# Hybrid decoder layer: the second tile's inverse applied once, gate z by tokens, stages moved

## The chip, the cores and the metric

The kernel runs on one core of a Trainium2 chip, in fp32, as one program. The metric is the device time in microseconds (us) of one execution. The engines are TensorE (PE), VectorE (DVE), ScalarE (ACT), GpSimd (POOL) and SyncE (SP), which issues most DMAs. Each has its own instruction queue, run in order, and waits on semaphores.

## The reference, cut to what matters

Batch 1, 256 tokens, width 2048, one layer. A mixing block projects the normed input to u and v (gMLP), to q, k, v and gate z of a gated DeltaNet of 16 heads of 128, to beta and a decay, and to two output gates; then come an output projection, a SwiGLU feed-forward (5632 wide), a per-layer embedding gate and a last norm.

```
h = rms_norm(x, norm_mix);  proj = h @ w_in
q, k, v = silu(causal_conv4(proj_qkv));  q, k = l2norm(q) * dk**-0.5, l2norm(k)
beta = sigmoid(dn_beta);  g = -exp(a_log) * softplus(dn_a + dt_bias)
# gated delta rule, chunks, g summed within a chunk
m    = strict_lower((k*beta) @ k.T * decay);  inverse = (1 + m)^-1
u_c  = inverse @ (v*beta);  w_c = inverse @ (k*beta*exp(g))
v_new = u_c - w_c @ state
o     = (q*exp(g)) @ state + (q @ k.T * decay) @ v_new
state = state*exp(g_last) + k_tail.T @ v_new
o = rms_norm(o, dn_out_norm) * silu(z)
merged = gate_a * (y_a @ w_a) + gate_b * (o @ w_b);  x = x + merged @ w_out
x = x + (silu(f_gate) * f_up) @ w_down;  x = x + ple_gate * (p @ w_ple);  rms_norm(x)
```

## The kernel before, in words

**Weights.** Every large matrix streams from HBM in *halves* of 512 KB, 604 in all, through a ring of four slots. For each half ACT makes a rounded high part (`split_hi`, L287) and DVE the remainder (`split_lo`, L295), three halves ahead of their use. TensorE multiplies the high weights by high and low activations at once (512 columns: 256 tokens high, 256 low) and the low weights by the high activations (256 columns). The result for columns of output features lies with features on partitions, its high and low sums side by side (`times_high` L302, `times_low` L307). With `rows=True` the tokens lie on partitions and the weights move, 512 wide (L320, L325): 12 matmuls for a half instead of 16. Where nothing else stands between them, halves go in pairs (`use_pair`): both high parts, then both low parts. A finished block leaves PSUM in two steps: ACT copies the low sum (`low_part`, L982), DVE adds the high sum (L1420), and for q, k, v, z DVE multiplies by R, the reciprocal root of the mean square of each token.

**Phases.** v (16 halves, tokens on partitions), then four head groups (`group`, 32 halves each: k, q, v, z of four heads, two blocks of four halves each), u (16), four rounds of mix (gate a, gate b, branch a, branch b), out, ffn, down, proj, ple. In phase v PE also makes the products for beta and decay (`beta_a`, L624, 16 fp32 matmuls on x times the norm's gain) behind half 12, and right behind it puts R on partitions (L628).

**The order of the small work** is written out by hand. `FINISH`, `START`, `CONV`, `EARLY` and `YS` are tables, one set for each engine: the number is the half of the running group behind which (PE) or with whose split (ACT, DVE) a stage stands. `START` holds stages of the group whose keys are just made, `FINISH` those of the group before. On ACT and DVE the split comes first, then the stages.

**Delta rule.** Two tiles of 128 tokens for each of four heads. PE makes the Gram matrices (`gram_m` L681, behind half 14), DVE scales them (`make_negm` L1521), ACT stores the 32x32 diagonal blocks and loads them back in another layout (`store_m`, `load_m` L1125), POOL inverts them in 62 small steps (`invert`, L509 and L511), ACT stores and loads the result (`store_x`, `load_diag`), and in the next group PE merges the blocks to the full inverse (`merge32_a` behind half 5, to `merge64_b` behind half 8). Then: `first_tile` behind 9 (inverse times weighted values, and inverse times weighted keys `kbeg`, four products each), `carry` behind 10, `second_tile` behind 11 (for each head inverse times values plus `nwT` times state), `outputs` behind 12. The outputs are squared (POOL), their root taken (ACT, `o_rt`), scaled (DVE, `o_scale` L1576, one instruction), turned (PE, `turn_o` L789, behind half 20), and multiplied by the gain and by silu(z) (DVE, `norm_o` L1583). The query-key product `gram_q` (L691) stands behind half 20 and waits for the query's SiLU (ACT L1036).

For the last group the finishing stages run in phase u and at the start of mix: `o_scale` with the last u half, `turn_o` behind mix half 0, the spatial products (`spatial`, L838) behind mix half 2.

Of the kernel before, what the change touches and what calls it, by code (L numbers as in the profile page):

```python
# [13 lines left out]


# [5 lines left out]
F32 = mybir.dt.float32  # L21
# [25 lines left out]
WARM = 16  # L47
# [30 lines left out]
E0, _e = {}, 0  # L78
for _name, _n in (("qkvz", 8 * NGROUPS), ("u", 4), ("mix", 4 * NB), ("ffn", 2 * FB)):
    E0[_name] = _e  # L80
    _e += _n
# [13 lines left out]
def build(nc, win, wba, wa, wb, wo, wgu, wd, wpg, wpp, xT_d, pT_d, cols_d, hv_d, gmw_d, gmb_d, fin_d, out_d):  # L95
# [33 lines left out]
    kbeg = shared("kbeg", [P, GROUP, P], F32, 40)  # L129
# [17 lines left out]
    nwT = shared("nwT", [P, GROUP, P], F32, 81)  # L147
    state = shared("state", [P, GROUP, P], F32, 83)
    vg = xT[:].rearrange("p k n -> p (k n)")[:, 0:TILES * GM].rearrange("p (m n) -> p m n", m=TILES)
    uT = shared("uT", [P, GMT, SEQ], F32, 28)  # L150
# [4 lines left out]
    wba_sb = shared("wba_sb", [P, KD, 48], F32, 62)  # L155
    g1 = shared("g1", [48, SEQ], F32, 71)
# [48 lines left out]
    def heads(flat, width):  # L205
# [15 lines left out]
    consts_made, wba_scaled = sem("consts_made"), sem("wba_scaled")  # L221
# [12 lines left out]
    q_meaned, k_turned, k_summed, k_rooted, v_weighed = (sem("q_meaned"), sem("k_turned"), sem("k_summed"), sem("k_rooted"),  # L234
                                                         sem("v_weighed"))
# [15 lines left out]
    z_scaled, z_silu, yb_hi, yb_lo = sem("z_scaled"), sem("z_silu"), sem("yb_hi"), sem("yb_lo")  # L251
# [48 lines left out]
    def times_high(o, s, kt, m, x, k, begin):  # L300

        nc.tensor.matmul(o, whi[:, s, kt, m * P:(m + 1) * P], x[:, k].rearrange("p q n -> p (q n)"), start=begin, stop=False,  # L302
                         skip_group_check=True)

    def times_low(o, s, kt, m, x, k, end):

        return nc.tensor.matmul(o[:, 0:SEQ], wlo[:, s, kt, m * P:(m + 1) * P], x[:, k, 0], start=False, stop=end,  # L307
                                skip_group_check=True)

    def use_half(pe, phase, i, n, buf, first, last, h, x, rows=False, into=acc):  # L310
# [16 lines left out]
        else:  # L327
            pe.wait_ge(hi_done, half_of(phase, i, n) + 1)
            for kt in range(HALF_K):
                for m in range(2):  # L330
                    times_high(acc[buf][:, m], s, kt, m, x, HALF_K * h + kt, first and kt == 0)
            pe.wait_ge(lo_done, half_of(phase, i, n) + 1)
            for kt in range(HALF_K):
                for m in range(2):
                    mm = times_low(acc[buf][:, m], s, kt, m, x, HALF_K * h + kt, last and kt == HALF_K - 1)
        mm.then_inc(half_used, 1)

    def use_pair(pe, phase, i, n, buf, first, last, h, x):

        for p in range(2):  # L340
            pe.wait_ge(hi_done, half_of(phase, i, n + p) + 1)
            for kt in range(HALF_K):
                for m in range(2):
                    times_high(acc[buf][:, m], (n + p) % RING, kt, m, x, HALF_K * (h + p) + kt, first and p == 0 and kt == 0)
        for p in range(2):
            pe.wait_ge(lo_done, half_of(phase, i, n + p) + 1)
            for kt in range(HALF_K):
                for m in range(2):
                    mm = times_low(acc[buf][:, m], (n + p) % RING, kt, m, x, HALF_K * (h + p) + kt,
                                   last and p == 1 and kt == HALF_K - 1)  # L350
            mm.then_inc(half_used, 1)
# [46 lines left out]
    with nc.Block() as block:  # L398
# [58 lines left out]
        def _(pool):  # L457
# [35 lines left out]

            pool.wait_ge(cols_in, 16)
            pool.wait_ge(ba_in, 32)
            g.tensor_tensor(wba_sb[:], wba_sb[:], bc(cols[:, C_MIX:C_MIX + KD], 48), ALU.mult).then_inc(wba_scaled, 1)

            INV_STEPS = 63

# [1417 lines left out]
```

## Time and profile before

| | us |
|---|---|
| median of 3 runs | 1814.24 (1812.48 to 1818.14) |
| the profiled execution | 1817.25 |
| its span | 1815.6 |
| DVE busy | 1166.4 (64%) |
| ACT busy | 882.1 (49%) |
| POOL busy | 257.5 (14%) |

```profile
## 2 busy tenths in 40 slices
PE   9999999999999999999999999999999999999998
PEld 8788888888888888888888888888888888888887
DVE  6587797787957655665667555555555555545556
ACT  6664454545546444444445444444444443434455
POOL 4016152161621000000010000000000000000002
PEclk9999999999999999999999999999999999999999
```

Each digit is one fortieth of the span (45 us), in tenths; PEclk is the clock that was granted to TensorE. The head groups lie in slices 2 to 12; from about 600 us on only the large products are left. A matmul's own span overlaps the next one's, so a stretch of PE is measured from start to start.

### The profile page before, as it was taken

The numbers are of one execution on the slowest core, as the hardware profiler recorded it, in microseconds if no ns is written. First come the engines' busy times: TensorE is split into PE (matmuls) and PEld (weight loads), VectorE is DVE, ScalarE is ACT, GpSimd is POOL, SyncE is SP. The second block draws the span as 40 slices with busy tenths as digits, with TensorE's granted clock in tenths as the row PEclk, the third lists the DMA queues.
The fourth block names the chain that finished last, engine by engine and source line by source line (L and its number), as shares of the span: only waits on it lengthen the run. The fifth ranks groups of instructions, "written<-read, shape, count | busy, mean of one in ns | idle before, by whom it ended". The sixth has DMA issues, their size and how long they took to land.

```text
span 1815.6 us, 29811 instructions
## 1 busy us (share of the span) xinstructions
PE 1794.4 (99%) x10662; PEld 1580.9 (87%) x10662; DVE 1166.4 (64%) x1415; ACT 882.1 (49%) x1040; POOL 257.5 (14%) x367
## 2 busy tenths in 40 slices
PE   9999999999999999999999999999999999999998
PEld 8788888888888888888888888888888888888887
DVE  6587797787957655665667555555555555545556
ACT  6664454545546444444445444444444443434455
POOL 4016152161621000000010000000000000000002
PEclk9999999999999999999999999999999999999999
DMA  7456456464565565555555555555555556565653
GB/s 256 156 173 188 143 155 192 129 189 139 176 188 188 188 195 192 180 190 196 176 184 195 190 191 192 189 190 185 186 192 188 185 184 203 172 206 175 224 180 130
DMA packets 103848, 332.64 MB, mean 183 GB/s; under 512 B 23184, under 2 KB 23328, under 8 KB 103520
## 3 DMA queue, kind: packets, MB, share of 16 engines
q1 hardware_dynamic: 88592, 320.57, 54.0%
q10 hardware_dynamic: 14096, 5.07, 1.3%
q0 software_dynamic: 1088, 6.03, 0.9%
q8 instruction: 47, 0.77, 0.2%
q14 instruction: 25, 0.20, 0.0%
HBM read 328.46 MB, written 3.16 MB: 183 GB/s over the span
## 4 chain that ended last, share of the span: by engine, by line
PE 88%; DVE 6%; issue 2%; ACT 2%; ACTq 1%; DVEq 0%; DMA 0%; POOL 0%; POOLq 0%
PE acc L302 50%; PE acc L307 26%; PE acc L320 4%; PE acc L325 2%; DVE wlo L295 2%; ACT whi L287 1%; DVE negm L1521 0%; PE acc L916 0%; PE acc L915 0%; PE acc L914 0%; DVE conv_k L1452 0%; DVE conv_q L1452 0%; PE ps L646 0%; PE ps L624 0%; DVE pre L1420 0%
## 5 line engine op out<-in xcount | busy, mean ns | idle before, releaser
L295 DVE TENSOR_TENSOR wlo<-raw,whi 128x1024 fp32r<-128x1024 f32 x604 | 750.0, 1267 | 517.4 <-ACT whi L287 513.6
L287 ACT ACTIVATE whi<-raw 128x1024 fp32r<-128x1024 f32 x604 | 623.7, 1055 | 579.9 <-PE acc L307 504.7
L302 PE MATMUL acc<-ax,whi 128*128 128x512 f32 x3072 | 754.5, 394 | 0.9 <-ACTq L1178 0.9
L302 PEld LDWEIGHTS acc<-ax,whi 128*128 128x128 f32 x3072 | 560.4, 189 | 106.9 <-ACTq L1178 1.1
L307 PEld LDWEIGHTS acc<-ax,wlo 128*128 128x128 f32 x3072 | 404.6, 191 | 22.0 <-DVE wlo L295 0.4
L307 PE MATMUL acc<-ax,wlo 128*128 128x256 f32 x3072 | 411.2, 283 | 0.0
L302 PE MATMUL acc<-fx,whi 128*128 128x512 f32 x704 | 172.5, 392 | 0.0
L302 PEld LDWEIGHTS acc<-fx,whi 128*128 128x128 f32 x704 | 128.0, 189 | 23.6
L565 POOL TENSOR_TENSOR sqsum<-sqsum,t 128x512 f32<-128x512 f32 x16 | 22.1, 1380 | 632.2 <-ACT t L1307 632.2
L307 PEld LDWEIGHTS acc<-fx,wlo 128*128 128x128 f32 x704 | 93.5, 191 | 5.3
L509 POOL TENSOR_TENSOR blk_t<-blk_m,blk_x 128x60 f32<-128x60 f32 (+24 forms) x124 | 71.3, 575 | 169.3 <-DMA blk_m<-inv_in 159.9
L307 PE MATMUL acc<-fx,wlo 128*128 128x256 f32 x704 | 95.1, 283 | 0.0
L573 POOL TENSOR_TENSOR t<-t,R 128x512 f32<-128x512 f32 x22 | 28.7, 1305 | 449.5 <-ACT t L1320 449.5
L320 PE MATMUL acc<-whi,ax 128*128 128x512 f32 x320 | 81.6, 398 | 0.0
L320 PEld LDWEIGHTS acc<-whi,ax 128*128 128x128 f32 x320 | 60.9, 192 | 12.6
L511 POOL TENSOR_TENSOR blk_x<-blk_x,blk_t 128x60 f32<-128x60 f32 (+24 forms) x124 | 66.3, 535 | 9.7
L302 PE MATMUL acc<-mx,whi 128*128 128x512 f32 x256 | 62.6, 392 | 0.0
L302 PE MATMUL acc<-yb,whi 128*128 128x512 f32 x256 | 61.4, 391 | 0.0
L1420 DVE TENSOR_TENSOR t<-acc,t 128x512 f32<-128x512 f32 x80 | 54.7, 684 | 10.4 <-ACT t L982 10.4
L982 ACT ACTIVATE t<-acc 128x512 f32<-128x512 f32 x80 | 47.5, 594 | 22.6 <-PE acc L307 19.3
L302 PEld LDWEIGHTS acc<-yb,whi 128*128 128x128 f32 x256 | 46.9, 188 | 9.0
L302 PEld LDWEIGHTS acc<-mx,whi 128*128 128x128 f32 x256 | 46.6, 189 | 8.6
(273 smaller groups left out, 1342.9 us busy)
## 6 DMA issues: line engine op xcount, KB each, us to landing
raw<-in_win SPq DMA_DIRECT2D x224, 512.0 KB, 3.6
raw<-in_wgu SPq DMA_DIRECT2D x176, 512.0 KB, 4.1
raw<-in_wd SPq DMA_DIRECT2D x88, 512.0 KB, 4.0
raw<-in_wb SPq DMA_DIRECT2D x32, 512.0 KB, 4.0
raw<-in_wo SPq DMA_DIRECT2D x32, 512.0 KB, 4.4
raw<-in_wpg SPq DMA_DIRECT2D x32, 512.0 KB, 3.6
raw<-in_wa SPq DMA_DIRECT2D x16, 512.0 KB, 4.7
blk_m<-inv_in ACTq DMA_DIRECT2D x16, 128.0 KB, 4.3
```

Source lines behind the costliest of these rows:

```text
L287: nc.scalar.activation(whi[:, s], raw[:, s], ACT.Copy).then_inc(hi_done, 1)
L295: nc.vector.tensor_tensor(wlo[:, s], raw[:, s], whi[:, s].bitcast(F32), ALU.subtract).then_inc(lo_done, 1)
L302: nc.tensor.matmul(o, whi[:, s, kt, m * P:(m + 1) * P], x[:, k].rearrange("p q n -> p (q n)"), start=begin, stop=False, skip_group_check=True)
L307: return nc.tensor.matmul(o[:, 0:SEQ], wlo[:, s, kt, m * P:(m + 1) * P], x[:, k, 0], start=False, stop=end, skip_group_check=True)
L320: nc.tensor.matmul(into[buf][:, m], x[:, WIDE_K * h + kt, q, m * P:(m + 1) * P], whi_w[:, s, kt], start=first and kt == 0 and q == 0, stop ...
L325: mm = nc.tensor.matmul(into[buf][:, m], x[:, WIDE_K * h + kt, 0, m * P:(m + 1) * P], wlo_w[:, s, kt], start=False, stop=last and kt == WI ...
L509: chain(g.tensor_tensor(tmp, blk_m[:, j + 1:32, j:j + 1].to_broadcast([P, r, c]), blk_x[:, j:j + 1, 0:c].to_broadcast([P, r, c]), ALU.mult ...
L511: chain(g.tensor_tensor(blk_x[:, j + 1:32, 0:c], blk_x[:, j + 1:32, 0:c], tmp, ALU.add), v + 3 + 2 * j)
L565: g.tensor_tensor(sqsum[:], sqsum[:], piece(t[1], q % 2), ALU.add).then_inc(s["added"], 1)
L573: g.tensor_tensor(piece(t[1], j), piece(t[0], j), over(R[:], 2), ALU.mult).then_inc(ff_gate, 1)
L982: f(dst, accv[buf][:, :, 1], ACT.Copy).then_inc(low_taken, 1)
L1420: v.tensor_tensor(dst, accv[buf][:, :, 0], dst, ALU.add).then_inc(part_summed, 1)
```

## The change

- *Second tile.* `kbeg`, `nwT` and their products are gone. The keys of the second tile are copied aside by POOL (`keep_k`); a new stage `keys_state` behind half 11 multiplies them by the state, DVE adds that times a (now negative) weight to the weighted values (`less_state`), and `second_tile`, now behind half 12, applies the inverse once. `outputs` goes to 13.
- *Gate z* is computed with tokens on partitions (`rows=True`, weights laid out so on the host), in two blocks that each cover half of the input width, added by DVE. SiLU takes R as its scale; `o_scale` multiplies by root and gate in eight instructions; `norm_o` becomes a scaled copy on ACT, behind the turn.
- *Beta* in the split format: ACT and DVE split the small weights, PE makes 16 matmuls of 512 columns and 112 rows on the split activations; R's columns come before half 12 instead of behind the beta product.
- *Pairs* take turns in which part goes first; *warm-up* is 5 matmuls of 512 columns instead of 16 of 64.
- *Stages moved*, as the tables show.

```diff
-WARM = 16
+WARM = 5
-                mm(psf[1][:, 64 * n:64 * n + 64], ones[:], ones[:, 0:64], start=True, stop=True)
+                mm(ps[1][:, n % 2], ones[:], over(ones[:], 4), start=True, stop=True)
...
-            for n in range(0, halves - 1, 2):
-                    use_pair(pe, phase, i, n0 + n, buf, n == 0, n + 2 == halves, n, x)
+            for n in range(0, halves - 1, 2):
+                    use_pair(pe, phase, i, n0 + n, buf, n == 0, n + 2 == halves, n, x, low_now())
+        if low_first:
+            low(first, False)
+            high(False, last)
+        else:
+            high(first, False)
+            low(False, last)
+    def low_now():
+        return next(turns) % 2 == 1
...
-                pe.wait_ge(wba_scaled, 1)
+                pe.wait_ge(wba_split, 2)
                 for k in range(KD):
-                    last = mm(psf[1][0:48, 0:SEQ], wba_sb[:, k], xT[:, k], start=(k == 0), stop=(k == KD - 1))
+                    last = mm(ps[1][0:112, 0], wsp[:, k], ax[:, k].rearrange("p q n -> p (q n)"), start=(k == 0), stop=(k == KD - 1))
+            def r_columns():
                 pe.wait_ge(r_done, 1)
...
+            def keep_k(n):
+                pool.wait_ge(conv_silu, n)
+                g.tensor_copy(kend[:], conv[1][:, :, P:SEQ]).then_inc(k_kept, 1)
...
             def first_tile(d):
...
-                for h in range(GROUP):
-                    last = mm(psq[1][:, 4 + h], kbeg[:, h], invT[:, 4 + h], start=True, stop=True)
+            def keys_state(d):
+                pe.wait_ge(k_kept, d + 1)
+                pe.wait_ge(delta_dve, 2 * d + 1)
+                for h in range(GROUP):
+                    last = mm(psq[1][:, 4 + h], kend[:, h], state[:, h], start=True, stop=True)
             def second_tile(d):
                 pe.wait_ge(delta_dve, 2 * d + 2)
                 for h in range(GROUP):
-                    mm(psq[0][:, 4 + h], invT[:, 4 + h], vbeta[:, 4 + h], start=True, stop=False)
-                    last = mm(psq[0][:, 4 + h], nwT[:, h], state[:, h], start=False, stop=True)
+                    last = mm(psq[0][:, 4 + h], invT[:, 4 + h], vbeta[:, 4 + h], start=True, stop=True)
+            def less_state(d):
+                for h in range(GROUP):
+                    x = v.scalar_tensor_tensor(vbeta[:, 4 + h], psq[1][:, 4 + h], kr[:, 2, 1, h:h + 1], vbeta[:, 4 + h], ALU.mult, ALU.add)
...
@@ tables of TensorE
-                      11: second_tile, 12: outputs, 20: turn_o}
-            EARLY = {20: gram_q}
-            START = {12: turn_k, 14: gram_m, 27: lambda g: (turn_q(g), transpose_v(g))}
+                      11: keys_state, 12: second_tile, 13: outputs, 22: turn_o}
+            EARLY = {22: gram_q}
+            START = {13: turn_k, 15: gram_m, 28: lambda g: (turn_q(g), transpose_v(g))}
+                    if p < 6:
+                        gemm("qkvz", g, p * HID, HID, p % 2, p // 2, ax, after=after)
+                    else:
+                        gemm("qkvz", g, p * HID, HID, p % 2, p // 2, ax, rows=True, after=after, h0=(p - 6) * HID)
-            gemm("v", 0, HWIDE, HWIDE, 1, 0, ax, rows=True, after={1: first_sum, 4: beta_a})
+            gemm("v", 0, HWIDE, HWIDE, 1, 0, ax, rows=True, after={1: first_sum, 3: r_columns, 4: beta_a})
-            mix(0, after={0: lambda: turn_o(NGROUPS - 1), 2: spatial})
+            mix(0, after={1: lambda: turn_o(NGROUPS - 1), 2: spatial})
@@ tables of ScalarE
-            FINISH = {1: (silu_z1,), 2: (store_x,), 3: (load_diag,), 6: (copy_p32,), 7: (copy_inv,), 10: (copy_v0,), 12: (copy_v1,),
-                      13: (copy_o,), 15: (o_rt,)}
-            START = {10: (silu_k,), 11: (decay_m,), 13: (square_k,), 15: (k_root,), 16: (store_m,), 17: (load_m,), 18: (silu_q,),
-                     20: (g_exp, decay_q), 25: (silu_v,), 28: (square_q,), 29: (silu_z0,)}
+            FINISH = {1: (silu_z,), 2: (store_x,), 3: (load_diag,), 6: (copy_p32,), 7: (copy_inv,), 10: (copy_v0,), 13: (copy_v1,),
+                      14: (copy_o,), 16: (o_rt,), 23: (norm_o,)}
+            START = {10: (silu_k,), 11: (decay_m,), 14: (square_k,), 16: (k_root,), 17: (store_m,), 18: (load_m, silu_q),
+                     20: (g_exp, decay_q), 25: (silu_v,), 29: (square_q,)}
+                if b == 3:
+                    act.wait_ge(o_mean, 3 * NGROUPS - 2)
-            YS = {0: (lambda: yb_high(1),), 1: (lambda: yb_high(2),), 5: (lambda: ya_high(0),),
+            YS = {0: (lambda: o_rt(NGROUPS - 1), lambda: yb_high(1)), 1: (lambda: yb_high(2),), 2: (lambda: norm_o(NGROUPS - 1),), 5: (lambda: ya_high(0),),
-                if n == 14:
+                if n == 13:
+                    ba_part()
                     v_block(0)
@@ VectorE
+                for h in range(GROUP):
+                    for m in range(TILES):
+                        o = t[2][:, h, m * P:(m + 1) * P]
+                        x = v.scalar_tensor_tensor(o, o, length[:, 2, 2 * h + m:2 * h + m + 1], zt[:, m, h * P:(h + 1) * P],
+                                                   ALU.mult, ALU.mult)
-                      9: (copy_invT64,), 10: (copy_nwT,), 11: (copy_state,), 14: (o_inv,), 18: (o_scale,), 21: (norm_o,)}
-            START = {10: (diff_m,), 14: (k_scale,), 15: (make_negm,), 17: (diff_q,), 22: (decay_q,), 25: (make_qkT,), 28: (scale_v,),
-                     29: (q_mean,)}
-            CONV = {5: conv_a(1, 0), 8: conv_b(1, 0), 14: conv_a(0, 1), 16: conv_b(0, 1), 21: conv_a(2, 2), 24: conv_b(2, 2)}
+                      9: (copy_invT64,), 11: (copy_state,), 12: (less_state,), 15: (o_inv,), 18: (o_scale,)}
+            START = {10: (diff_m,), 15: (k_scale,), 16: (make_negm,), 17: (diff_q,), 22: (decay_q,), 24: (make_qkT,), 29: (scale_v,),
+                     30: (q_mean,)}
+            CONV = {5: conv_a(1, 0), 9: conv_b(1, 0), 14: conv_a(0, 1), 16: conv_b(0, 1), 21: conv_a(2, 2), 24: conv_b(2, 2)}
-                if n == 15:
-                    o_scale(NGROUPS - 1)
-            YS = {0: (lambda: yb_low(1),), 1: (lambda: norm_o(NGROUPS - 1),), 3: (sv_bias,),
+            YS = {0: (lambda: yb_low(1), lambda: o_scale(NGROUPS - 1)), 3: (sv_bias,),
```

## Rows read from the trace of the kernel before

**Rows 1.** Busy times of the whole span: busy us (share of the span) xinstructions, by engine.

```profile
PE 1794.4 (99%) x10662; PEld 1580.9 (87%) x10662; DVE 1166.4 (64%) x1415; ACT 882.1 (49%) x1040; POOL 257.5 (14%) x367
```

**Rows 2.** Waits of TensorE: line waited for, us in total, times, longest us.

```profile
PE ps L691 <- ACT conv_q L1036: 6.8, 4, 4.0
PE ps L752 <- DVE invT L1554: 1.3, 3, 0.4
...
PE ps L838 <- DVE oT L1583: 1.0, 1, 1.0
PE acc L302 <- ACTq L1178: 0.9, 1, 0.9
```

**Rows 3.** Timeline of TensorE, phase v: start us, us, engine, line, operation.

```profile
21.39 1.98 PE L320 MATMUL acc<-whi,ax 128*128 128x512 f32 x8
...
24.11 1.98 PE L320 MATMUL acc<-whi,ax 128*128 128x512 f32 x8
```

**Rows 4.** Timeline of TensorE, last u block and first mix half, columns.

```profile
559.97 2.00 PE L302 MATMUL acc<-ax,whi 128*128 128x512 f32 x8
...
562.76 1.03 PE L789 MATMUL ps<-ident,t 128*128 128x128 f32 x8
```

**Rows 5.** Timeline of TensorE in the feed-forward, pairs of halves.

```profile
1034.54 3.82 PE L302 MATMUL acc<-ax,whi 128*128 128x512 f32 x16
...
1040.10 1.09 PE L302 MATMUL acc<-ax,whi 128*128 128x512 f32 x4
```

**Rows 6.** Timeline of TensorE, the beta product.

```profile
46.87 7.11 PE L624 MATMUL ps<-xT,wba_sb 128*48 128x256 f32 x32
```

**Rows 7.** Timeline of ScalarE, the root that makes R.

```profile
44.80 0.42 ACT L977 ACTIVATE R<-Rt 128x256 f32<-128x256 f32 x1 [2.26 <-DVE Rt L1402]
```

**Rows 8.** Timeline of TensorE, group 2, second tile and the half behind it.

```profile
322.17 0.39 PE L769 MATMUL ps<-vbeta,invT 128*128 128x128 f32 x2
...
323.87 1.40 PE L302 MATMUL acc<-ax,whi 128*128 128x512 f32 x5
```

**Rows 9.** Timeline of VectorE, group 2, half 12 and the scaled Gram matrix.

```profile
324.44 1.22 DVE L295 TENSOR_TENSOR wlo<-raw,whi 128x1024 fp32r<-128x1024 f32 x1
...
344.31 2.16 DVE L1521 SCALAR_TENSOR_TENSOR negm<-ps,kr,negm 128x128 f32<-128x128 f32 x8
```

**Rows 10.** Timeline of TensorE, group 2, query-key product and transpose.

```profile
355.21 2.05 PE L691 MATMUL ps<-conv_q,conv_k 128*128 128x128 f32 x16 [0.60 <-ACT conv_q L1036]
357.58 1.09 PE L789 MATMUL ps<-ident,t 128*128 128x128 f32 x8 [0.32 <-DVE t L1576]
```

**Rows 11.** Timeline of TensorE, group 0, the query-key product.

```profile
129.75 3.78 PE L691 MATMUL ps<-conv_q,conv_k 128*128 128x128 f32 x16 [3.97 <-ACT conv_q L1036]
```

**Rows 12.** Stretch behind it: us, busy PE PEld DVE ACT POOL, PEclk, DMA share, GB/s.

```profile
130.00:136.00 6.00, 6.00 (x23) 5.42 (x24) 3.82 (x5) 5.88 (x7) 5.04 (x11) 0.51 0.60 182
```

**Rows 13.** Timeline of ScalarE, group 0, issue of the block loads.

```profile
124.42 1.75 ACTq L1125 DMA_DIRECT2D blk_m<-inv_in  x4
```

**Rows 14.** Timeline of ScalarE, last u block.

```profile
558.51 1.28 ACT L1110 ACT_TABLE_LOAD   x1
...
565.40 1.05 ACT L1239 ACTIVATE yb<-oT 128x1024 fp32r<-128x1024 f32 x1
```

**Rows 15.** Timeline of ScalarE, group 2, issue of the block loads.

```profile
349.79 1.74 ACTq L1125 DMA_DIRECT2D blk_m<-inv_in  x4
```

**Rows 16.** Timeline of GpSimd, group 2, from the blocks' arrival to the diagonal's.

```profile
356.06 2.64 POOL L509 TENSOR_TENSOR blk_t<-blk_m,blk_x 128x31 f32<-128x31 f32 x1 [23.09 <-DMA blk_m<-inv_in]
...
364.28 0.27 POOL L509 TENSOR_TENSOR blk_t<-blk_m,blk_x 128x52 f32<-128x52 f32 x1
...
408.12 1.45 POOL L518 COPY invT<-diagT 32x256 f32<-32x256 f32 x1 [10.65 <-DMA diagT<-inv_out]
```

**Rows 17.** Timeline of TensorE, first merge behind group 2.

```profile
408.10 1.07 PE L713 MATMUL ps<-diagT,negm 32*32 32x32 f32 x32
```

**Rows 18.** Timeline of VectorE, group 2, o_scale.

```profile
356.24 1.22 DVE L1576 TENSOR_TENSOR t<-t,length 128x1024 f32<-128x1024 f32 x1
```

More of the change, by code:

```diff
@@ L327, in use_half @@
         else:
[L328 to L335, printed above, removed]
-        mm.then_inc(half_used, 1)
@@ L338, in use_pair, with high @@
[L338 to L351, printed above, removed]
+            def high(begin, end):
+                pe.wait_ge(hi_done, half_of(phase, i, n) + 1)
+                for kt in range(HALF_K):
+                    for m in range(2):
+                        mm = times_high(acc[buf][:, m], s, kt, m, x, HALF_K * h + kt, begin and kt == 0, end and kt == HALF_K - 1)
+                return mm
@@ new lines, in low @@
+            def low(begin, end):
+                pe.wait_ge(lo_done, half_of(phase, i, n) + 1)
+                for kt in range(HALF_K):
+                    for m in range(2):
+                        mm = times_low(acc[buf][:, m], s, kt, m, x, HALF_K * h + kt, begin and kt == 0, end and kt == HALF_K - 1)
+                return mm
+            if low_first:
+                low(first, False)
+                mm = high(False, last)
+            else:
+                high(first, False)
+                mm = low(False, last)
@@ new lines, in use_half, with use_pair, high, low @@
+        mm.then_inc(half_used, 1)
+    def use_pair(pe, phase, i, n, buf, first, last, h, x, low_first):
+        def high(begin, end):
+            for p in range(2):
+                pe.wait_ge(hi_done, half_of(phase, i, n + p) + 1)
+                for kt in range(HALF_K):
+                    for m in range(2):
+                        mm = times_high(acc[buf][:, m], (n + p) % RING, kt, m, x, HALF_K * (h + p) + kt,
+                                        begin and p == 0 and kt == 0, end and p == 1 and kt == HALF_K - 1)
+                if low_first:
+                    mm.then_inc(half_used, 1)
+        def low(begin, end):
+            for p in range(2):
+                pe.wait_ge(lo_done, half_of(phase, i, n + p) + 1)
+                for kt in range(HALF_K):
+                    for m in range(2):
+                        mm = times_low(acc[buf][:, m], (n + p) % RING, kt, m, x, HALF_K * (h + p) + kt,
+                                       begin and p == 0 and kt == 0, end and p == 1 and kt == HALF_K - 1)
+                if not low_first:
+                    mm.then_inc(half_used, 1)
+        if low_first:
+            low(first, False)
+            high(False, last)
+        else:
+            high(first, False)
+            low(False, last)
@@ L353, in acc_free @@
+    turns = itertools.count()
+    def low_now():
+        return next(turns) % 2 == 1
     def acc_free(pe, phase, i, buf, n):
```

165 lines of the change are left out of this document (98 added, 67 removed).

## The prediction

> **What bounds the kernel now.** I read the page's busy times first, then TensorE's waits, then its timeline. TensorE (PE) works for 1794.4 of 1815.6 us [rows 1]: the time is the sum of its matmuls, and a change pays only if it takes matmul time out of PE or closes one of its gaps. The gaps in the middle are few: 6.8 us before the query-key product of the four head groups, 1.3 before the first-tile product, 1.0 before the spatial products, 0.9 at a buffer [rows 2]. What the change does on VectorE (DVE), ScalarE (ACT) and GpSimd (POOL) counts only through such gaps. The profiled execution took 1817.25 us (span 1815.6); the median of the runs is 1814.24, 3.0 lower. I sum against 1817.25 and take the same difference from 1814.24. Halves (512 KB of weights) are numbered within a head group, 0 to 31; "on the old clock" means in the times of the trace.
>
> **A half.** With rows of tokens it takes 24.11-21.39 = 2.72 us [rows 3], with columns 562.76-559.97 = 2.79 [rows 4], in a pair 1040.10-1034.54 = 5.56, 2.78 each [rows 5]. A switch between high and low products costs about 0.01.
> - *Gate z by tokens:* 32 halves x 0.07 = **-2.3**.
> - *Pairs that take turns in which part comes first:* 159 pairs lose one of two switches, -1.7. A low-first pair needs its second low half 1 us after its start instead of 4.6 us; no row shows such a half late, but behind a block's evacuation it is the last thing that DVE makes. Between a loss of 2 and all of the 1.7, I take **-1.0**.
>
> **The beta product.** Sixteen fp32 products took 7.04 us [rows 6]. Sixteen of 512 columns in the split format, at the rate of rows 3 (2.72/12 = 0.227), take 3.6: -3.4. But the columns of R now come ahead of half 12 of this phase, which began at 46.87-2.8 = 44.1, and R is there only at 45.22, released by DVE and not by PE [rows 7]: +1.2. With an extra stage switch of 0.1 the sum is **-2.1**. This wait also absorbs what the five wide warm-up products do to the start: between 1.5 late and 2.5 early, both are gone at 45.2. The first value block's activation moves one half earlier on ACT, so the buffer of [rows 2] is free 3 us sooner: its 0.9 goes, with 0.1 of restart, **-1.0**.
>
> **Second tile.** Eight products take 323.87-322.17 = 1.70 us [rows 8], so four fewer save 0.85, less a stage switch of 0.1: four times 0.8 is -3.2. Against it stands a new wait. Keys times state would end at 322.17+0.85 = 323.0 on the old clock and half 12 at 325.9; the four products behind it wait for the subtraction, which DVE begins after the split that ends at 325.66. Four instructions of L1521's kind (2.16/8 = 0.27 each) make it 326.8 [rows 9]: 0.9, four times, +3.6 (0 were DVE ahead, 4.5 were they slower). Behind the waiting products stands only PE's own queue, so all of it is time. Net **+0.3** with rounding. The first-tile product waits for a copy that now comes before the key convolution on DVE instead of behind it: 1.3 us in three groups [rows 2] plus restarts, **-1.8**.
>
> **The query-key product** moves from behind half 20 to behind half 22, 5.6 us. In groups 1 to 3 the 2.8 us of wait go. The product also stretches there, 357.58-355.21 = 2.37 for what takes 1.70, the transpose's 0.32 within it [rows 8, 10]; I count 0.7 for each: **-5.0**. In group 0 the wait was 3.97 us [rows 11], and the clock granted behind it 0.51, the lower level of 1.2 GHz, for 6 us [rows 12]: 3 us of work lost. Those 7.0 go. But between its splits for halves 21 and 22 ACT now issues the block loads and runs the query's SiLU. The issue began at 124.42 and took 1.75 [rows 13]. Its input is now made behind an evacuation and a split more on DVE (1.4 and 1.2, by columns from rows 9) and without kbeg (-0.7), so 126.3. With 1.75, a table load of 1.28, the SiLU and the split, 1.05 each [rows 14], half 22 has its high part at 131.4; PE wants it at 129.75-3.97+2.8 = 128.6. That is +2.8, or 1.4 if the stores land faster; I take 2.3, too short to bring the clock down. Net **-4.7**.
>
> **The inversion's chain.** From the load's issue at 349.79 [rows 15] the chain runs through POOL (from 356.06) to the diagonal blocks at 408.12 [rows 16], and PE starts on them at 408.10 [rows 17]: no slack in this group. The change makes the load 1.0 to 1.9 us later here (the count of group 0; I take 1.0, since DVE is not filled throughout) and PE 2.2 earlier (gaps closed 1.6, z 0.6): 3.2 us of new wait per group, if POOL stays as slow. It doesn't quite: POOL's first step took 2.64 us while DVE ran tensor_tensors such as L1576 [rows 18], against 0.27 beside convolutions of scalar_tensor_tensors [rows 16]. The change turns L1576 (1.22) into eight of the latter and drops two z scalings (1.4), so up to 2.6 come back. I take 0.8 in group 2 and 0.3 each in groups 1 and 3: **+1.4**, between 0 and 10.
>
> The Trainium skill, "SBUF — State Buffer", section "Who interferes with whom", says that any VectorE instruction with two inputs in SBUF keeps GpSimd's reads out, not only a tensor_tensor. By it the eight new o_scale instructions would block POOL for 2.2 us where the old one took 1.2, the chain would be some 2 us longer than in my sum in two groups, and the saving 4 us smaller. The trace speaks against it with the steps of 0.27 us beside convolutions that read SBUF twice.
>
> **The last group's outputs.** Here the change costs. turn_o moves one half on, to 562.76+2.79 = 565.55 on the old clock [rows 4]. The scaling that it waits for moves further: the outputs are made a half later, o_rt follows the last u block's GELU and a split on ACT, with a table load, and o_scale on DVE stands behind yb_low(1), which waits for yb_high(1) on ACT. yb_high(1) began at 565.40 behind the same GELU and split; a table load of 1.28 and the root (0.2) now come before it: from 566.9 to 568.0 [rows 14]. DVE's yb_low(1), as wide as L1576, adds 1.2 [rows 18] and o_scale 8 x 0.27 = 2.15 [rows 9]: 571.3. PE waits 571.3-565.5 = 5.8 us. A wait of 3.97 lowered the clock and cost 3.0 more [rows 11, 12]; I add 3.0. The 1.0 before the spatial products goes [rows 2], since norm_o is on ACT, half a stage ahead of them. Net **+7.8**, between -1.1 (scaling in time) and +9.
>
> **Sum.** -2.3 -1.0 -2.1 -1.0 +0.3 -1.8 -5.0 -4.7 +1.4 +7.8 = -8.4 us: 1817.25 becomes 1808.9 in a profiled execution, 1814.24 becomes 1805.8. The z scaling, kbeg, nwT and norm_o that leave DVE and the key copy that POOL gets are put at nothing: PE's matmuls cover them, as they cover the 1166.4 us that DVE is busy [rows 1]; POOL's copy stands ahead of square_o and ends before its input is there. Without that cover the copy would cost its 0.7 to 1.4 per group.
>
> **Rivals.**
> - *A, the last outputs come in time* (a wait under 2 us, clock untouched): 7 to 9 us better, 1797.5. For it: ACT's and DVE's queues have idle time there. Against it: both run in order, and yb_high(1) already began at 565.40. 0.24.
> - *B, POOL gives the chain nothing back:* 3 x 3.2 instead of 1.4, 8.2 worse, 1814.0. For it: no slack at 408.10. Against it: 2.64 against 0.27 [rows 16]. 0.16.
> - *C, slower: the clock falls at the chain.* The place is PE's wait for diagT behind half 5 of each group. At 3.2 us it stands 0.8 short of the wait of rows 11; if the load comes 1.9 later instead of 1.0, it passes it, and each of three waits costs 0.9 and 3.0 more: 1814.0+11.7 = 1825.7. 0.08.
> - *D, the second SBUF input blocks POOL* (eight instructions of 0.27): 1805.8+4.2 = 1810. Against it: the 0.27 of rows 16. It is the skill's rule of the section named above. 0.07.
> - *The forecast*, 1800 to 1809.5: 0.45.
>
> **The numbers.** 0.3%, 5.4 us, is about what a measurement can tell from no change, so the limits are 1808.8 and 1819.7. Faster: A and most of the forecast, 0.69. Same: B, D, the forecast's edge, 0.22. Slower: C and what I don't see, 0.09. The range takes in the better part of A and all of B: 1794 to 1814.5.
>
> **What would show it.** Right: L691 is gone from TensorE's waits or below 0.5; there is one wait of 5 to 6 us near 560 before the transpose of the last outputs, with a granted clock of half behind it; 0.9 four times before the second tile, on DVE's subtraction; 1.2 before the columns of R; 1.4 to 3 for a high half in group 0; z halves at 2.72. Wrong: no wait before that transpose (A); merge32_a waiting 3 us for its transfer in three groups (B), with half a clock behind it (C); low halves waited for in the pairs.

## The result

The changed kernel takes 1807.09 us (median of 5 runs, 1804.78 to 1808.35), the kernel before beside it 1817.38 (median of 5). The ratio is 0.9947, with a 95% interval of 0.9928 to 0.9966. The profiled execution took 1808.35 us against 1817.25, 8.9 less; 8.4 was forecast.

Busy times of the whole span, which answer to [rows 1]:

```profile
PE 1782.1 (99%) x10464; PEld 1563.5 (87%) x10464; DVE 1169.4 (65%) x1442; ACT 887.1 (49%) x1041; POOL 251.6 (14%) x371
```

TensorE is busy for 12.3 us less and waits 3.4 us more. Its waits, which answer to [rows 2] (line waited for, us in total, times, longest us):

```profile
PE ps L839 <- DVE t L1657: 6.2, 1, 6.2
PE ps L820 <- DVE vbeta L1639: 3.4, 4, 0.8
PE ps L759 <- DMA diagT<-inv_out: 1.6, 2, 1.4
PE acc L329 <- DVE wlo L299: 1.4, 1, 1.4
PE acc L324 <- ACT whi L291: 1.3, 2, 1.1
...
PE ps L674 <- ACT R L1032: 1.1, 1, 1.1
```

The query-key product's wait of 6.8 us is gone. In its place stand 6.2 before the last transposes, four of 0.8 before the second tile, and 1.6 for the diagonal blocks. At the start, 1.3 for high halves and 1.1 for R (L324, L674) take in whatever differs before them, and 1.4 for a low half (L329) lies in group 0.

**The sum, term by term.** All 4880 high products stand in the same order in both traces, so I compared the starts of the same halves and gave what exceeds an undisturbed half to the product or wait beside it (times in us):

| term | forecast | measured |
|---|---|---|
| gate z by tokens | -2.3 | -2.3 |
| pairs that take turns | -1.0 | -1.6 |
| beta product, with the wait for R | -2.1 | -1.8 |
| buffer of the first value block | -1.0 | -1.1 |
| second tile | +0.3 | +1.2 |
| first tile's copy | -1.8 | -2.4 |
| query-key product, groups 1 to 3 | -5.0 | -6.1 |
| query-key product, group 0 | -4.7 | -5.7 |
| the inversion's chain | +1.4 | +3.2 |
| the last group's outputs | +7.8 | +7.9 |
| sum | -8.4 | -8.7 |

The starts of the last halves differ by 8.9; the rest is rounding and what no term names.

The timeline of TensorE (start us, us, engine, line, operation) gives each term. A gate half with tokens as rows takes 140.73-138.01 = 2.72, as [rows 3]:

```profile
138.01 1.98 PE L324 MATMUL acc<-whi,ax 128*128 128x512 f32 x8
...
140.73 1.98 PE L324 MATMUL acc<-whi,ax 128*128 128x512 f32 x8
```

The columns of R wait for ACT, then half 12 and the beta product in the split format follow; 52.74-49.06 = 3.68 stands against the 7.04 of [rows 6]:

```profile
45.67 0.60 PE L674 MATMUL ps<-ones,R 1*128 1x1 f32 x4 [1.06 <-ACT R L1032]
...
49.06 3.84 PE L667 MATMUL ps<-ax,wsp 128*112 128x512 f32 x16
52.74 1.98 PE L324 MATMUL acc<-whi,ax 128*128 128x512 f32 x8
```

In group 2, keys times state takes 0.81, and the second tile's products come 0.85 late; they answer to [rows 8]. The column in brackets is the wait before the row:

```profile
310.30 1.05 PE L813 MATMUL ps<-state,kend 128*128 128x128 f32 x8
...
315.00 1.16 PE L820 MATMUL ps<-vbeta,invT 128*128 128x128 f32 x8 [0.85 <-DVE vbeta L1639]
```

On VectorE the split of step 12 (L299) stands ahead of the subtraction, which ends at 314.94 (compare [rows 9]):

```profile
312.69 1.21 DVE L299 TENSOR_TENSOR wlo<-raw,whi 128x1024 fp32r<-128x1024 f32 x1
313.83 1.11 DVE L1639 SCALAR_TENSOR_TENSOR vbeta<-ps,kr,vbeta 128x128 f32<-128x128 f32 x4
```

In group 0 the query-key product starts without a wait ([rows 11]: 3.97):

```profile
127.96 1.95 PE L737 MATMUL ps<-conv_q,conv_k 128*128 128x128 f32 x16
```

ScalarE issued the block loads at 119.79 and ran the query's SiLU at 122.87 ([rows 13]: 124.42 for the issue):

```profile
119.79 1.76 ACTq L1183 DMA_DIRECT2D blk_m<-inv_in  x4
...
122.87 1.06 ACT L1094 ACTIVATE conv_q<-conv_q 128x1024 f32<-128x1024 f32 x1
```

The first inversion's diagonal blocks come 1.38 late, in the second group. The high half behind them takes 180.54-177.12 = 3.42 instead of 1.96; in that stretch the granted clock is 0.62 on the mean (columns as in [rows 12]), since it stood at 0.5, the lower level of 1.2 GHz, from 176.9 to 180.3:

```profile
176.05 1.14 PE L759 MATMUL ps<-diagT,negm 32*32 32x32 f32 x32 [1.38 <-DMA diagT<-inv_out]
177.12 3.58 PE L306 MATMUL acc<-ax,whi 128*128 128x512 f32 x8
180.54 1.11 PE L311 MATMUL acc<-ax,wlo 128*128 128x256 f32 x8
```

```profile
176.00:180.50 4.50, 4.45 (x40) 3.73 (x41) 4.50 (x10) 2.06 (x5) 2.77 (x4) 0.62 0.45 146
```

Before the last transposes TensorE waits 6.19. They take 558.39-556.77 = 1.62 instead of 0.79 and the half behind them 3.56 instead of 1.94, at half the clock, for 6.8 us in all:

```profile
556.77 1.97 PE L839 MATMUL ps<-ident,t 128*128 128x128 f32 x8 [6.19 <-DVE t L1657]
558.39 3.76 PE L306 MATMUL acc<-ax,whi 128*128 128x512 f32 x8
```

On ScalarE the root (L1168) stands behind the GELU, a split and a table load, and yb_high(1) (L1308) behind it; on VectorE yb_low(1) (L1773) is ahead of the eight scalings (L1657), which end at 556.7. This is the chain that the prediction drew from [rows 14]:

```profile
550.91 1.28 ACT L1168 ACT_TABLE_LOAD   x1
552.20 0.21 ACT L1168 ACTIVATE length<-length 128x8 f32<-128x8 f32 x1
552.32 1.04 ACT L1308 ACTIVATE yb<-oT 128x1024 fp32r<-128x1024 f32 x1
```

```profile
553.39 1.23 DVE L1773 TENSOR_TENSOR yb<-oT,yb 128x1024 fp32r<-128x1024 f32 x1 [1.24 <-ACT yb L1308]
554.53 2.18 DVE L1657 SCALAR_TENSOR_TENSOR t<-t,length,xT 128x128 f32<-128x128 f32 x8
```

### The profile page after: what moved, and what is told of

It is laid out like the page before. It is cut to its first block, busy times and chain, and to the rows that moved or that the text cites. A ratio compares the mean times of both kernels' runs of the same rounds, so it can differ in the third digit from the quotient of the medians.

```text
span 1806.7 us, 29541 instructions
## 1 busy us (share of the span) xinstructions
PE 1782.1 (99%) x10464; PEld 1563.5 (87%) x10464; DVE 1169.4 (65%) x1442; ACT 887.1 (49%) x1041; POOL 251.6 (14%) x371
## 4 chain that ended last, share of the span: by engine, by line
PE 89%; issue 2%; DVE 2%; POOL 2%; DMA 2%; ACT 1%; ACTq 0%; POOLq 0%; DVEq 0%; SPq 0%
PE acc L306 49%; PE acc L311 26%; PE acc L324 6%; PE acc L329 3%; DMA raw<-in_win 1%; POOL blk_x L544 1%; DVE wlo L299 1%; POOL blk_t L542 1%; ACT whi L291 1%; DMA inv_out<-blk_xT 0%; PE acc L971 0%; PE acc L970 0%; PE acc L969 0%; DMA diagT<-inv_out 0%; PE ps L737 0%
## 5 line engine op out<-in xcount | busy, mean ns | idle before, releaser
L299 DVE TENSOR_TENSOR wlo<-raw,whi 128x1024 fp32r<-128x1024 f32 x604 | 749.4, 1265 | 513.8 <-ACT whi L291 507.7
L306 PE MATMUL acc<-ax,whi 128*128 128x512 f32 x2816 | 682.4, 394 | 0.0
L306 PEld LDWEIGHTS acc<-ax,whi 128*128 128x128 f32 x2816 | 518.7, 189 | 101.4
L311 PEld LDWEIGHTS acc<-ax,wlo 128*128 128x128 f32 x2816 | 363.1, 191 | 15.1
L311 PE MATMUL acc<-ax,wlo 128*128 128x256 f32 x2816 | 367.6, 283 | 0.0
L324 PE MATMUL acc<-whi,ax 128*128 128x512 f32 x576 | 143.9, 392 | 1.3 <-ACT whi L291 1.3
L324 PEld LDWEIGHTS acc<-whi,ax 128*128 128x128 f32 x576 | 107.0, 188 | 24.6 <-ACT whi L291 2.2
L329 PE MATMUL acc<-wlo,ax 128*128 128x512 f32 x288 | 77.4, 391 | 1.4 <-DVE wlo L299 1.4
L542 POOL TENSOR_TENSOR blk_t<-blk_m,blk_x 128x60 f32<-128x60 f32 (+24 forms) x124 | 63.8, 514 | 102.0 <-DMA blk_m<-inv_in 92.6
L329 PEld LDWEIGHTS acc<-wlo,ax 128*128 128x128 f32 x288 | 53.8, 188 | 13.8 <-DVE wlo L299 2.7
```

Of the source, the lines that this page charges most:

```text
L299: nc.vector.tensor_tensor(wlo[:, s], raw[:, s], whi[:, s].bitcast(F32), ALU.subtract).then_inc(lo_done, 1)
L306: return nc.tensor.matmul(o, whi[:, s, kt, m * P:(m + 1) * P], x[:, k].rearrange("p q n -> p (q n)"), start=begin, stop=end, skip_group_ch ...
L324: nc.tensor.matmul(into[buf][:, m], x[:, WIDE_K * h + kt, q, m * P:(m + 1) * P], whi_w[:, s, kt], start=first and kt == 0 and q == 0, stop ...
L329: mm = nc.tensor.matmul(into[buf][:, m], x[:, WIDE_K * h + kt, 0, m * P:(m + 1) * P], wlo_w[:, s, kt], start=False, stop=last and kt == WI ...
L542: chain(g.tensor_tensor(tmp, blk_m[:, j + 1:32, j:j + 1].to_broadcast([P, r, c]), blk_x[:, j:j + 1, 0:c].to_broadcast([P, r, c]), ALU.mult ...
```

## The experiments

Every kernel but the last two is the changed kernel with one edit. Whole times of one kernel spread by up to 4.6 us (1799.57 to 1804.21 for the second experiment). The traces also differ at the start (R's wait is between 0.7 and 1.1) and in the first inversion, for a reason that stays open below. So what an edit does is read at its place, from the starts of the same halves, and the medians stand beside it.

### The last scaling early

```
 ScalarE, last u block:   u_part(3)
+                         o_rt(NGROUPS - 1)
                          u_block(3)
 VectorE:                 u_block(3)
+                         o_scale(NGROUPS - 1)
 (both taken out of step 0 of the first mix)
```

> From the changed kernel (1808.35 us profiled); only the last head group's root and scaling are issued earlier: the root ahead of the last u block's GELU on ACT, the scaling right behind that block's evacuation on DVE. Theory (the wait of 6.19 us before the last transposes comes from the order in ACT's and DVE's queues, and the low clock behind it from the wait): the input of the root is there at 546.7, ACT is free at 547.1, a table load and the root end at 548.6, the evacuation at 549.3, eight scalings end at 551.5, and TensorE is there at 550.6: the wait becomes 0.9 and the 2.75 us of low clock go, -8.0 us. Rival 1 (the low clock belongs to the eight short transposes and the spatial products, not to the wait): -5.3. Rival 2 (the split behind the GELU, now a table load later, takes the wait's place): -3 to -5.

Measured: 1798.37 us, ratio to the kernel before 0.9895 (0.9879 to 0.9912). At its place it saves 8.05 us. The wait is 0.84. The root ends at 548.0, a table load is paid twice, and the scalings, begun at 548.60, end at 550.8:

```profile
546.51 1.28 ACT L1168 ACT_TABLE_LOAD   x1
547.80 0.21 ACT L1168 ACTIVATE length<-length 128x8 f32<-128x8 f32 x1
548.03 1.28 ACT L1301 ACT_TABLE_LOAD   x1
```

```profile
548.60 2.18 DVE L1658 SCALAR_TENSOR_TENSOR t<-t,length,xT 128x128 f32<-128x128 f32 x8
```

No low clock follows, so the 2.75 us of low clock belonged to the wait. The order of two queues, not their load, cost the change half of what it could have given.

### The last transposes one half later

```
-mix(0, after={1: lambda: turn_o(NGROUPS - 1), 2: spatial})
+mix(0, after={2: lambda: turn_o(NGROUPS - 1), 3: spatial})
 (norm_o on ScalarE and the bias on VectorE one half later as well)
```

> From the changed kernel; nothing is made earlier, but TensorE transposes the last outputs one half later (and the spatial products, ACT's norm and DVE's bias move with it). Theory (the scaling is ready at 556.7 whatever TensorE does): TensorE comes 2.8 us later, the wait is 3.4 instead of 6.19, -2.8; the low clock behind it, 2.75 us, stays, since a wait of 4.2 us brought it in the kernel before. Rival (the clock falls only behind the longer wait): -5.5. Either way the norm on ACT must not delay a split; if it does, up to 1 us is lost again.

Measured: 1803.07 us, ratio 0.9915 (0.9899 to 0.9932), -3.9 at its place, between the two. (The wait of the kernel before, 4.2 in the expectation, is 3.97 in [rows 11].) The wait is 3.40, as forecast, and the clock does fall behind it, but for 3.4 us instead of 6.8: the transposes take 1.62 as before, the half behind them 2.69 instead of 3.56.

```profile
556.57 1.97 PE L839 MATMUL ps<-ident,t 128*128 128x128 f32 x8 [3.40 <-DVE t L1657]
558.19 2.85 PE L306 MATMUL acc<-ax,whi 128*128 128x512 f32 x8
```

### Pairs without turns

```
 def low_now():
-    return next(turns) % 2 == 1
+    return False
```

> From the changed kernel; in the pairs of halves the high products always come first, as before the change. Theory (a change between high and low products costs 0.01 us each, and there are 159 pairs): +1.6 us, spread evenly from 565 us to the end, which is what the two traces differ by there. Rival (the 1.6 us comes from other things behind 565): 0.

Measured: 1807.51 us, ratio 0.9943 (0.9926 to 0.9959). Between the first pair and the end it loses 1.65 us to the changed kernel. All of the term comes from the switches, and no low half was waited for.

### The subtraction ahead of its split

```
 for n in range(GH):
+    if n == 12:
+        less_state(g - 1)
     split_lo(dve, "qkvz", g, n)
 (the same in phase u for the last group; taken out of step 12)
```

> From the changed kernel; DVE makes the subtraction for the second tile ahead of the split of half 12 instead of behind it, in all four groups. Theory (the 0.85 us that TensorE waits before the second tile is DVE's order: the split of 1.21 stands ahead of the subtraction, and its result is not wanted before 3 us later): the four waits go, -3.4 us. Rival (DVE is the limit there, and the wait moves to the low half behind): 0.

Measured: 1802.25 us, ratio 0.9915 (0.9898 to 0.9931). The second tile's wait is gone from the list of waits, and the stage costs 0.90 instead of 2.00 in each group: -4.4. That is 1.0 more than the four waits of 0.85: each wait costs 0.25 beside its own length, 0.10 of it in the product behind it.

### The columns of R behind the beta product

```
-after={1: first_sum, 3: r_columns, 4: beta_a}
+after={1: first_sum, 3: beta_a, 4: r_columns}
 (ScalarE's v_block(0) from step 13 to 14, VectorE's copy of R behind its step for beta)
```

> From the changed kernel; TensorE makes the beta product ahead of the columns of R instead of behind them, and ACT's activation of the first value block goes back one half. Theory (two terms of the sum hang together): the wait for R, 0.8 to 1.1 us in the five traces so far, is covered by the product's 3.7 us and goes; the value block's buffer comes free a half later and the buffer wait of the kernel before, 1.0 with its restart, is back: 0.0 in sum. Rival (the buffer wait went for another reason): -1.0 us.

Measured: 1806.35 us, ratio 0.9943 (0.9926 to 0.9961). The wait for R is gone (-1.1 at half 13), and the buffer's is back, 1.0 before half 4 of group 0; with restarts the kernel stands 0.3 behind the changed one at half 12 of that group. The two terms hang together. What came on top was not expected: group 0 then lost 1.2 us more, and in the second group the wait for the diagonal blocks fell to 0.3, with no low clock, so that the trace ends 2.0 before the changed kernel's:

```profile
PE acc L306 <- ACTq L1244: 1.0, 1, 1.0
...
PE ps L759 <- DMA diagT<-inv_out: 0.3, 1, 0.3
```

### The first inversion's store early

```
 for n in range(GH):
+    if n == 16:
+        make_negm(0)
     split_lo(dve, "qkvz", 0, n)
```

> From the changed kernel; in the first head group alone DVE makes the matrix that is stored for the inversion ahead of the split of half 16 instead of behind it. Theory (TensorE's wait of 1.4 to 1.7 us for the diagonal blocks in the second group, and the low clock of 3.4 us behind it, come from the first group's inversion, whose chain begins at this store): the store and all behind it come 1.2 us earlier, the wait shrinks to 0.2 to 0.5 and the low clock is gone: -1.2 -1.5 = -2.7 us. Rival 1 (the low clock needs no wait of this size): -1.2. Rival 2 (the chain is paced by ACT's place in its queue, not by the store): 0.

Measured: 1807.06 us, ratio 0.9953 (0.9937 to 0.9968). The four loads were issued at 119.90 (119.79 in the changed kernel), and one of the four issues took 1.8 us instead of 0.45; ScalarE's split behind it came late and TensorE waited 1.8 for it. The inversion ended at 163.6 instead of 166.4, since its 62 steps took 35.6 us instead of 37.2, and the wait for the diagonal blocks went with its low clock (-3.0 in the second group). Group 0 lost 2.5, so the net is -0.5 at these places. So the low clock does hang on that wait, but the edit didn't move the load, as the second rival had it.

### The second key convolution back

```
-CONV = {5: conv_a(1, 0), 9: conv_b(1, 0), ...
+CONV = {5: conv_a(1, 0), 8: conv_b(1, 0), ...
```

> From the changed kernel; the second key convolution goes back from behind step 9 to behind step 8 on DVE, so that the copy of the inverse for the first tile waits behind it again. Theory (the first tile's 1.7 us in the kernel before against 0.9 were this wait): +0.8 in three head groups, +2.4 us. Rival (the copy would be in time anyway): 0.

Measured: 1806.68 us, ratio 0.995 (0.9932 to 0.9969), which tells nothing by itself. At its place the first tile costs 0.50, 0.70 and 0.69 more in the three groups, with waits of 0.25 to 0.44: +1.9. The move accounts for 1.9 of the 2.4 measured. Most of the other 0.5 is no wait for this copy: in the last group, where TensorE waited for nothing there, the stage is shorter too, by 0.9 for the four products that the term counts at 0.8.

### The query-key product back

```
-EARLY = {22: gram_q}
+EARLY = {20: gram_q}
```

> From the changed kernel; TensorE's query-key product goes back from behind half 22 to behind half 20, everything else as changed. Theory (most of the 11.8 us that this step gave comes from ACT's and DVE's order, which has the query's activation ready at 123.9, 235.1, 343.8 and 452.8, and not from TensorE's move): TensorE would be there at 122.4, 234.9, 343.7 and 452.7: waits of 1.6, 0.2, 0.1 and 0.1, and one stage switch of 0.09 more in three groups, together +2.3 us. Rival (the move on TensorE is what gave it): +8 us or more, with the low clock back in the first group.

Measured: 1805.94 us, ratio 0.994 (0.9919 to 0.996). TensorE waits 1.47, 0.06 and 0.22 there, and no low clock follows. Over halves 20 to 29 that is +0.3, +0.3, +0.5 and +0.3: 1.4 of the 11.8 us. The other 10.4 came from what this run left as changed. On ScalarE and VectorE that is the order: in group 0 the SiLU began at 128.64 in the trace of before, and at 122.87+2.97 = 125.84 on the same clock in the changed kernel. On TensorE it is the two stages of transposes that also stand later (turn_o behind half 22, those of the query and the value behind half 28). The share of each step was not tried. As a whole the kernel came out 2.4 faster than the changed one: the first inversion ended 3.9 earlier (162.5), its wait with the low clock was gone (-3.0), and the start was 0.6 earlier.

### Every split on VectorE as a scalar_tensor_tensor

```
-tensor_tensor(wlo, raw, whi, subtract)
+scalar_tensor_tensor(wlo, whi, -1.0, raw, mult, add)
```

> From the changed kernel; every split on DVE is one scalar_tensor_tensor (high part times -1 plus the weights) instead of one tensor_tensor, of the same 1024 elements, with the same two inputs in SBUF. Theory (as in the prediction: a tensor_tensor keeps GpSimd out, a scalar_tensor_tensor doesn't): the steps of the inversion beside a split fall from 0.9 us to 0.36, the 37.2 us from its first to its last step to about 28, and the wait for the diagonal blocks in the second group goes with its low clock, -3 us, if the split itself is not slower. Rival (any DVE instruction with two inputs in SBUF keeps GpSimd out as long as it runs, and the steps beside the convolutions are short because each of those runs for 0.4 us only): the steps stay at 0.9 and the inversion at 37, 0 us.

Measured: 1804.73 us, ratio 0.9933 (0.9912 to 0.9955). The mean of GpSimd's steps that lie mostly beside a split is 0.91 us (85 steps; 0.92 over 83 in the changed kernel), and the first inversion takes 37.2 us, as before. In the timelines of VectorE and GpSimd two steps beside the six convolutions, of 0.48 us each, take 0.38 and 0.40, and the one that meets the long scalar_tensor_tensor takes 1.24:

```profile
251.24 2.88 DVE L1529 SCALAR_TENSOR_TENSOR conv_v<-pre,cols,conv_v 128x256 f32<-128x256 f32 x6
254.04 1.36 DVE L299 SCALAR_TENSOR_TENSOR wlo<-whi,raw 128x1024 fp32r<-128x1024 f32 x1
```

```profile
253.46 0.38 POOL L544 TENSOR_TENSOR blk_x<-blk_x,blk_t 128x64 f32<-128x64 f32 x1
253.92 0.40 POOL L542 TENSOR_TENSOR blk_t<-blk_m,blk_x 128x75 f32<-128x75 f32 x1
254.40 1.24 POOL L544 TENSOR_TENSOR blk_x<-blk_x,blk_t 128x75 f32<-128x75 f32 x1
```

The rival holds: what counts is that two inputs lie in SBUF, and how long the instruction runs. Beside L1583 of the kernel before, a scalar_tensor_tensor of 1.28 us with one input in PSUM, nine steps took 0.29 on the mean. (Of the 3.9 us that this trace ends earlier than the changed kernel's, 2.1 are the second group, where the wait was 0.6 with no low clock, and 1.4 lie behind the last transposes, where the low clock began 4 us before the wait's end instead of 1.)

### The old warm-up

```
-WARM = 5, products of 512 columns
+WARM = 16, products of 64 columns
```

> From the changed kernel; the warm-up is again 16 narrow products instead of 5 wide ones. Theory (what the warm-up gives to the start is absorbed by the wait for R, which DVE releases): the first half starts at 8.0 on the lower clock, 3.56 us for its high products, the full clock comes near 13, and half 13 still starts at 52.4 to 52.8, 0.0 us. Rival (the wide warm-up gives the start 2.3 us): +2.3 us.

Measured: 1806.58 us, ratio 0.9941 (0.9921 to 0.9961). The full clock comes at 10.4 instead of 6.2, the first high products take 3.02 instead of 1.93, and half 13 starts at 52.28: 52.74 in the changed kernel, 51.87 to 52.36 in the four kernels of the first experiments, which start as it does. Its trace ends 2.2 before the changed kernel's: half 13 came 0.5 earlier, group 0 lost 1.75, and the second group's wait for the diagonal blocks was gone with its low clock (-3.0). The edit was not aimed at these. The warm-up gives nothing that the wait for R doesn't take.

### Three fixes together

The last scaling early, the subtraction ahead of its split, and the query-key product behind half 20; then the same with that product behind half 21.

> From the changed kernel (1808.35 us profiled); the last scaling early, the subtraction ahead of its split, and the query-key product behind half 20, together. Theory (the three act in different places and add up): -8.1 -4.3 -2.4 = -14.8, 1793.5 us profiled, with one wait of 0.8 before the last transposes, 1.5 before the first group's query-key product, none before the second tile, and no low clock until the last microseconds. Rival (TensorE, 1.1 us earlier in each group, meets the inversion's chain again): one to three waits of 1 us before the diagonal blocks, with low clock behind them, 1796 to 1800.

> As the run with the three fixes, but the query-key product stands behind half 21. Theory (the query's activation is ready at 123.9 in the first group and TensorE is there at 125.2; the wait of 1.5 goes, but DVE, which caught up in that wait, is then late for half 27 again, and the first inversion's load meets the traffic that it met with the product behind half 22): 0 to +3 us against the three fixes. Rival (only the wait counts): -1.4 us against them.

Measured: 1793.72 us (1793.55 to 1794.10), ratio 0.987 (0.9851 to 0.989), and 1793.06 us, ratio 0.9865 (0.9845 to 0.9884). The first is 14.8 below the changed kernel at the last halves, as forecast; both beat both kernels. What is left of TensorE's waits in the first: the query's SiLU, high halves at the start, the warm-up's ones and the last scaling, and 0.8 for R.

```profile
PE ps L737 <- ACT conv_q L1094: 1.8, 3, 1.5
...
PE ps L839 <- DVE t L1658: 0.8, 1, 0.8
```

The second is 0.2 below it in the traces and 0.7 in the medians. In group 0 neither place is better: the wait of 1.5 is gone and 1.5 for a low half at half 27 has come. In groups 1 to 3 half 21 is the better place by 0.4 each; a start that came 0.8 later hides most of this in the whole trace. Neither the theory (0 to +3) nor the rival (-1.4) had it.

## Why the prediction was right

The time was right within 0.5 us of the profiled difference (8.4 against 8.9; in medians 1805.8 against 1807.09), and so was the mechanism of its biggest term. The terms behind it were off by up to 1.8, and that they cancelled is luck.

- **The last outputs** (+7.8; 7.9): wait 6.2 against 5.8, low clock 2.75 against 3.0. The wait and its cause are shown by the early scaling, which takes back 8.05, and the clock's share by the disappearance of the low clock with it. Rival A was wrong because ScalarE and VectorE kept the order in which the steps were issued, though both had idle time; the same idle time made it cheap to mend.
- **Gate z, buffer, beta** were right within 0.3. That R's wait absorbs the start is shown by the old warm-up, and that it stands against the buffer by the swap.
- **Pairs** (-1.0; -1.6): all switches paid and no low half was late. The doubt that I priced at 0.7 didn't come true.
- **Second tile** (+0.3; +1.2): four waits of 0.85 were forecast at 0.9, and its cause is shown. With the wait closed the term is 1.2-4.4 = -3.2, which is what I had for the products; what I missed is the 0.25 that each wait costs beside its length.
- **First tile, query-key in groups 1 to 3** (-6.8 together; -8.5): the query's and value's transposes behind half 27 also lost a stretch, 1.4 us over the three groups, 0.8 of it a wait of the kernel before in group 1 (for qkT, L1536); I had not counted it.
- **Group 0** (-4.7; -5.7): here a step failed. "The issue ... so 126.3" on the old clock was 119.79+2.97 = 122.8: earlier than before, not later. There was no wait for half 22's high part. Instead VectorE, with no pause above 0.2 from 134.7 to 146.8, was 1.4 late with the low part of half 27, and the two errors left 1.0.
- **The inversion's chain** (+1.4; +3.2): two errors. I took group 2, with no slack in the trace of before, for the place; it was the first inversion, which had 4.9 us of slack (it ended at 168.0, ScalarE stored it at 172.9). TensorE came 9.2 us earlier there and the load only 4.6, and from the issue to the end of the last copy it took 3.0 longer (end 166.4): 1.7 from the issue to GpSimd's first step (7.46 against 5.75), 0.3 in the steps (37.23 against 36.97) and 1.0 in the copy. ScalarE's store, which had waited for its place in the queue, now waited for the copy:

```profile
167.32 0.70 POOL L513 COPY blk_xT<-blk_x 128x256 f32<-128x256 f32 x1 [0.17 <-POOL blk_x L511]
172.89 2.65 ACTq L1133 DMA_DIRECT2D inv_out<-blk_xT  x4
```

```profile
164.64 1.74 POOL L546 COPY blk_xT<-blk_x 128x256 f32<-128x256 f32 x1 [0.17 <-POOL blk_x L544]
166.49 2.66 ACTq L1191 DMA_DIRECT2D inv_out<-blk_xT  x4
```

The first pair is from the kernel before, the second from the changed one. And a wait of 1.4 did bring the clock down, where I had called 2.3 "too short to bring the clock down" in group 0; that doubled the price. Rival C had the mechanism, but in three groups and behind longer waits. In group 2 I had set 3.2 of new wait against what GpSimd gives back. There the load was issued 0.6 later on the old clock, but GpSimd began at 345.33+10.75 = 356.08 against 356.06, and its steps took 1.6 less; a wait of 0.2 is all that came.

The second error is the reading of [rows 16]. I said that a scalar_tensor_tensor lets GpSimd pass and a tensor_tensor doesn't. The run with long scalar_tensor_tensors shows that it doesn't. In the kernel before, the step of 2.64 stood beside L1576 [rows 18] and a split right behind it. The step of 0.27 at 364.28 began as one short instruction of the convolution ended and the next began:

```profile
357.37 1.21 DVE L295 TENSOR_TENSOR wlo<-raw,whi 128x1024 fp32r<-128x1024 f32 x1
...
363.67 0.68 DVE L1449 TENSOR_SCALAR conv_v<-pre,cols 128x256 f32<-128x256 f32 x2
364.28 1.90 DVE L1452 SCALAR_TENSOR_TENSOR conv_v<-pre,cols,conv_v 128x256 f32<-128x256 f32 x4
```

Beside all of these short scalar_tensor_tensors a step takes 0.37 on the mean (55 steps) against 0.26 with VectorE idle, so they do cost GpSimd something, but little. What the long ones show is the rule of the Trainium skill, "SBUF — State Buffer", section "Who interferes with whom", which I had weighed as rival D and given 0.07; the runs agree with it. Turning L1576 into eight short instructions helped where it had blocked: in group 2 GpSimd's first step took 1.64 instead of 2.64, since it met the last of the eight (0.36) and the split behind it (1.23) in place of L1576 and its split. That is a matter of the length of the pieces, not of their kind. The inversions of groups 1, 2 and 3 took 1.1, 1.6 and 2.7 us less from first to last step, against the 2.6 that I had as the most, so case B was rightly no more than a rival.

What stays open is why the first inversion's steps take 35.4 to 35.6 us in four of the traces and 36.8 to 37.6 in the nine others of the changed kernel and its variants. In those four TensorE waited 1.1 to 1.8 us between halves 20 and 22 of group 0, in the others less than 0.3; how the one leads to the other was not tried.

## What to carry to other kernels

When a step is moved on a kernel with in-order queues, write down for each engine what stands between its input and its output in the new order; the largest cost of this change, and its largest gain, were both such an order, and neither was work. Slack that a trace shows at one place is spent when another engine gets earlier, so the chain that was safe before is the first to check. And a wait behind which the clock falls can cost twice its length (1.4 and 1.5 more at the diagonal blocks), so it comes first on the list.

## What the runs showed of the hardware

- The granted clock does not follow from a wait's length alone. Of six waits of 1.38 to 1.71 us before the diagonal blocks, followed by 1.07 us of short products, five brought 3.4 us at half clock and one (1.45 us) none; waits of 1.4 to 1.75 before a low half of wide products brought none in any trace. A wait of 3.4 brought 3.4 us, one of 3.97 (the kernel before) 6.8. Each wait of 6.2 brought 6.8 too, but part of that can fall into the wait itself. In nine traces with this wait the low clock began 0.9 to 4.0 us before the wait's end, and the earlier it began the less it cost: 0.2 less than in the changed kernel (1.0 before the end) at 1.5, 0.5 less at 2.1, 1.0 less at 3.2 and 1.4 less at 4.0, the last in the run with scalar_tensor_tensor splits. My 3.0 for it was near for this execution only.
- VectorE pays for the contention too. In the changed kernel a split takes 1.44 us on the mean when an instruction of GpSimd runs beside any part of it (121 splits) and 1.22 when none does (483). Beside the short steps of the inversion alone it is 1.29 (59).
- Four DMA issues in a row take 1.74 us on ScalarE; in one run a single one of them took 1.8 instead of 0.45, and the split behind it was late.
